# A three-layer transformer block on one core: attention heads of two layers taken in pairs on the two halves of TensorE's rows

## What is computed

```
s_loc = einsum('bnqkgd,bnjkd->bnkgqj', qb, kw) * scale        # windowed; masked outside |q - k| <= 128
s_ctx = einsum('bnqkgd,bckd->bnkgqc', qb, kc) * scale
p = softmax(concatenate([s_loc, s_ctx, sink]))
o = einsum('bnkgqj,bnjkd->bnqkgd', p_loc, vw) + einsum('bnkgqc,bckd->bnqkgd', p_ctx, vc)
...
x_new = x + g1 * (concatenate([ya, yb, yc, yd]) @ w_out)      # yc windowed, yd global
```

## Time and profile before

| | us |
|---|---|
| median of 3 runs (lowest to highest) | 2987.54 (2985.93 to 2989.95) |
| the profiled execution | 2986.1 |
| its span | 2984.3 |
| TensorE busy | 2711.7 (91%) |
| VectorE busy | 1300.7 (44%) |
| ScalarE busy | 970.9 (33%) |
| POOL busy | 333.7 (11%) |
| mean granted TensorE clock | 0.943 |

### The profile page before, as it was taken

The page is one execution under the profiler, slowest core; times in us unless marked ns, Lnnn a source line. Parts: engine busy times, 40 slices in busy tenths (PEclk is TensorE's granted clock), DMA queues, the critical chain, the costliest instruction groups (busy, mean ns, idle before and its releaser), DMA issues.

```text
span 2984.3 us, 35383 instructions
## 1 busy us (share of the span) xinstructions
PE 2711.7 (91%) x13904; PEld 1548.5 (52%) x13904; DVE 1300.7 (44%) x2556; ACT 970.9 (33%) x1825; POOL 333.7 (11%) x185
## 2 busy tenths in 40 slices
PE   5999999699999998697897999998699997899998
PEld 3875554322333332585544333332277686787886
DVE  2496532434444444385523332232566555343342
ACT  4224431234344433524512222221324334322222
POOL 0210002001111111120010000000013321122221
PEclk9998989799999999797998999999899998999999
DMA  6216631599999999320024999999421002222221
GB/s 239 71 43 219 233 114 52 194 317 350 343 353 359 359 352 332 103 85 1 1 99 180 386 386 387 387 386 386 171 86 57 8 15 78 69 94 99 85 92 50
DMA packets 303260, 568.51 MB, mean 191 GB/s; under 512 B 12656, under 2 KB 55792, under 8 KB 302968
## 3 DMA queue, kind: packets, MB, share of 16 engines
q1 hardware_dynamic: 294480, 545.33, 51.5%
q0 software_dynamic: 3840, 12.59, 1.8%
q10 hardware_dynamic: 4776, 8.33, 0.8%
HBM read 551.53 MB, written 14.68 MB: 190 GB/s over the span
## 4 chain that ended last, share of the span: by engine, by line
PE 71%; DVE 6%; DMA 5%; ACT 3%; issue 2%; POOL 0%; ACTq 0%; DVEq 0%; SPq 0%
PE PS L958 21%; PE PS L964 6%; PE PS L907 5%; PE PS L1061 4%; PE PS L1060 4%; PE PS L1059 4%; PE PS L1072 2%; PE PS L1012 2%; PE PS L1074 2%; PE PS L1073 2%; PE PS L1049 2%; PE PS L725 2%; DMA WIDE<-in_w_gate_dram 1%; PE PS L883 1%; PE PS L870 1%
## 5 line engine op out<-in xcount | busy, mean ns | idle before, releaser
L958 PE MATMUL PS<-RING,RF 128*64 128x512 f32 x1448 | 353.5, 614 | 12.1 <-DMA RING<-in_w_up_dram 4.0
L958 PE MATMUL PS<-WIDE,RF 128*64 128x512 f32 x1408 | 331.9, 601 | 8.8 <-DMA WIDE<-in_w_up_dram 3.2
L2526 POOL TENSOR_TENSOR WHL<-RING,WHL 128x1024 fp32r<-128x1024 f32 x57 | 153.8, 2697 | 1240.7 <-ACT WHL L1292 1240.7
L958 PEld LDWEIGHTS PS<-RING,RF 128*64 128x64 f32 x1448 | 93.0, 138 | 221.6 <-issue 202.3
L1059 PE MATMUL PS<-RR,WHL 128*128 128x512 f32 x512 | 203.9, 398 | 1.1 <-DVE RR L2279 1.1
L1061 PE MATMUL PS<-RR,WHL 128*128 128x512 f32 x512 | 204.3, 399 | 0.0
L1060 PE MATMUL PS<-RR,WHL 128*128 128x512 f32 x512 | 202.0, 395 | 0.0
L958 PEld LDWEIGHTS PS<-WIDE,RF 128*64 128x64 f32 x1408 | 92.7, 137 | 203.9 <-issue 185.0
L1292 ACT ACTIVATE WHL<-RING 128x1024 fp32r<-128x1024 f32 (+1 forms) x115 | 119.7, 1045 | 176.2 <-PE PS L1074 101.9
L1523 ACT ACTIVATE RF<-PS,MODS,MSC 128x128 f32<-128x128 f32 x192 | 77.2, 437 | 302.9 <-PE PS L1012 156.1
L1775 DVE TENSOR_TENSOR WHL<-RING,WHL 128x1024 fp32r<-128x1024 f32 (+1 forms) x58 | 71.6, 1234 | 196.2 <-ACT WHL L1292 196.2
(11 more groups left out here) (383 smaller groups left out, 4997.2 us busy)
## 6 DMA issues: line engine op xcount, KB each, us to landing
RING<-in_w_gate_dram SPq DMA_DIRECT2D x83, 1024.0 KB
WIDE<-in_w_down_dram SPq DMA_DIRECT2D x74, 1024.0 KB, 8.2
RING<-in_w_up_dram SPq DMA_DIRECT2D x70, 1024.0 KB
WIDE<-in_w_up_dram SPq DMA_DIRECT2D x57, 1024.0 KB, 12.4
RING<-in_w_down_dram SPq DMA_DIRECT2D x51, 1024.0 KB
RING<-in_ada_w_dram SPq DMA_DIRECT2D x48, 1024.0 KB
WIDE<-in_w_gate_dram SPq DMA_DIRECT2D x45, 1024.0 KB, 11.2
RING<-in_w_in_dram SPq DMA_DIRECT2D x30, 1024.0 KB
```

The lines of the kernel that those rows point to most:

```text
L958: ins = e.matmul(a[r:r + 64, :], xs[:, j, 0:64], w[:, i, :], start=j < 2, stop=j > 5)
L2526: e.tensor_tensor(lo, load_buffer(loads[st["load"]])[:, js, cs], h.bitcast(F32), ALU.subtract).then_inc(pool, G(("lo", st["i"])))
```

## The change

Heads are taken as pairs (0, 2) and (1, 3), which lie on rows 0 to 63 and 64 to 127, and both score matmuls of a pair are issued next to each other. The plan goes by pairs: one turn n of the loop appends the head entry of items 2n and 2n + 1, sums of the pair before, flip of its first item, both middles, ada 0 and 1, one background entry that may take a bank, flip of its second item, ada 2, values of the pair before that, a background entry that in layer 1 may not take one of the ring's banks, ada 3. Statistics get six buffers. The output's halves now hold heads (0, 2) and (1, 3), for which the host lays out the rows of `w_out` in that order.

```diff
-    items = [(m, t, h) for m in range(2) for t in range(T if need_ctx else 4) for h in range(4)]
+    items = [(m, t, h) for m in range(2) for t in range(T if need_ctx else 4) for h in (0, 2, 1, 3)]
...
-        while need_ctx and now[0] % 2 == 0:
+        while need_ctx and now[0]:
             yield
...
-    for i in range(len(items) + 3):
...
+    pairs = len(items) // 2
+    for n in range(pairs + 2):
+        i = 2 * n
+        now[0] = 0
+        if 0 < n <= len(units):
+            plan.append(("ada", *units[n - 1], 4))
...
+        if n < pairs:
+            plan.append(("head", i, *items[i]))
+        if 0 < n <= pairs:
+            plan += [("sum", i - 2, *items[i - 2]), ("sum", i - 1, *items[i - 1]), ("flip", i - 2, *items[i - 2])]
+        if n < pairs:
+            plan += [("middle", i, *items[i]), ("middle", i + 1, *items[i + 1])]
+        if n < len(units):
+            plan += [("ada", *units[n], 0), ("ada", *units[n], 1)]
+        next(later, None)
+        if 0 < n <= pairs:
+            plan.append(("flip", i - 1, *items[i - 1]))
+        if n < len(units):
+            plan.append(("ada", *units[n], 2))
+        if n > 1:
+            plan.append(("values", i - 3, *items[i - 3]))
+        now[0] = 1
         next(later, None)
         if n < len(units):
+            plan.append(("ada", *units[n], 3))
...
-        STATS = [SM[:, 64 + 4 * i:68 + 4 * i] for i in range(4)]
+        STATS = [SM[:, 64 + 4 * i:68 + 4 * i] for i in range(6)]
...
-                        sc = bank(scores, ("score", l, i), (A, ("exp", l, i)))
+                        sc = [bank(scores, ("score", l, i + r), (A, ("exp", l, i + r))) for r in range(2)]
...
+                        for own in (True, False):
+                            for r in range(2):
+                                rs = slice(64 * r, 64 * r + 64)
+                                q = QKT[m][rs, h, 128 * t:128 * t + 128]
+                                if not own:
+                                    e.matmul(sc[r][:, 512:768], q, QKT[m][rs, 2, 512:768], start=True, stop=True
+                                             ).then_inc(pe, P(("score", l, i + r)))
+                                elif wl:
+                                    e.matmul(sc[r][:, 512 - wl:512], q, QKT[m][rs, 2, 128 * b0:128 * b1], start=True, stop=True)
...
-                        v0 = 512 * m + 384 + 64 * (h // 2)
+                        v0 = 512 * m + 384
...
-                                ins = e.matmul(o[64 * r:64 * r + 64, 0:128], QKV[:, b, v0:v0 + 64],
+                                ins = e.matmul(o[64 * r:64 * r + 64, 0:128], QKV[:, b, v0 + 64 * r:v0 + 64 * r + 64],
...
-                        if i > 3:
-                            e.wait_ge(pe, P["pv", l, i - 4 + (i + 1) % 2])
+                        if i > 5:
+                            e.wait_ge(pe, P["pv", l, i - 6 + (i + 1) % 2])
...
-                        e.tensor_tensor(YT2[:, 2 * m + h // 2, 128 * t:128 * t + 128], o[:, 0:128], SHARE[i // 2 % 2],
+                        e.tensor_tensor(YT2[:, 2 * m + h % 2, 128 * t:128 * t + 128], o[:, 0:128], SHARE[i // 2 % 2],
```

More of the change, by code:

```diff
@@ L269, in attention_plan @@
     nd = next(i for i, it in enumerate(items) if it[0] == 1)
-    for i in range(len(items) + 3):
-        now[0], n = i, i // 2
-        if i % 2 == 0 and 0 < n <= len(units):
+    pairs = len(items) // 2
[3 more added lines that the diff above has]
+        if 0 < n <= len(units):
             plan.append(("ada", *units[n - 1], 4))
-        if i % 2 and n < len(units):
-            plan.append(("ada", *units[n], 2))
         if i == nd:
@@ L278, in attention_plan @@
                 next(later)
[L279 to L282, removed]
+        if n < pairs:
[14 more added lines that the diff above has]
+        now[0] = 1
         next(later, None)
         if n < len(units):
-            plan.extend([("ada", *units[n], 3)] if i % 2 else [("ada", *units[n], q) for q in range(2)])
+            plan.append(("ada", *units[n], 3))
+    now[0] = 0
+    for _ in later:
+        pass
+    return plan
     for _ in later:
@@ L850, in attend @@
                         i, m, t, h = k
-                        rs, g = slice(64 * (h // 2), 64 * (h // 2) + 64), h % 2
-                        q = QKT[m][rs, g, 128 * t:128 * t + 128]
                         b0, b1 = span(m, t)
                         wl = 128 * (b1 - b0)
-                        sc = bank(scores, ("score", l, i), (A, ("exp", l, i)))
+                        sc = [bank(scores, ("score", l, i + r), (A, ("exp", l, i + r))) for r in range(2)]
                         e.wait_ge(act, A["qkT", l, m, 5])
[L857 to L860, removed]
+                        for own in (True, False):
[7 more added lines that the diff above has]
+                                    e.matmul(sc[r][:, 512 - wl:512], q, QKT[m][rs, 2, 128 * b0:128 * b1], start=True, stop=True)
                     elif what == "flip":
@@ L888, in attend @@
                             ins = e.matmul(o[64 * r:64 * r + 64, 128:256],
-                                           STATS[(i - 1 + r) % 4][:, 2:3].to_broadcast([128, 64]), IDN, start=True, stop=True)
+                                           STATS[(i - 1 + r) % 6][:, 2:3].to_broadcast([128, 64]), IDN, start=True, stop=True)
                         ins.then_inc(pe, P(("pv", l, i)))
@@ L1410, in attend @@
                         wl = 128 * (b1 - b0)
-                        st, eb = STATS[i % 4], EB[i % 3]
+                        st, eb = STATS[i % 6], EB[i % 3]
                         e.wait_ge(dve, V["neg", l, i])
@@ L2021, in attend @@
                         wl = 128 * (b1 - b0)
-                        sc, st = held("score", l, i), STATS[i % 4]
+                        sc, st = held("score", l, i), STATS[i % 6]
                         e.wait_ge(pe, P["score", l, i])
@@ L2030, in attend @@
                         e.wait_ge(dve, V.n)
-                        if i > 3:
-                            e.wait_ge(act, A["exp", l, i - 4])
+                        if i > 5:
+                            e.wait_ge(act, A["exp", l, i - 6])
                         e.tensor_reduce(st[:, 0:1], sc[:, 512 - wl:768], AX.X, ALU.max).then_inc(dve, V())
@@ L2051, in attend @@
                         i, m, t, h = k
-                        st = STATS[i % 4]
+                        st = STATS[i % 6]
                         if m == 0:
@@ L2701 @@
         rows += [g["q_norm_g"][l]] * 4 + [g["k_norm_g"][l]] * 2
+    by_half = [np.arange(64) + 64 * h for h in (0, 2, 1, 3)]
+    by_half = np.concatenate([np.arange(512)] + [512 + 256 * m + hr for m in range(2) for hr in by_half])
     con, hc, bias = tables()
@@ L2707 @@
         "consts": con, "hconst": hc, "bias": bias,
-        "x": g["x"][0], "ctxt": g["ctx"][0], "ada_w": g["ada_w"], "w_in": g["w_in"], "w_out": g["w_out"],
+        "x": g["x"][0], "ctxt": g["ctx"][0], "ada_w": g["ada_w"], "w_in": g["w_in"], "w_out": g["w_out"][:, by_half, :],
         "router": np.pad(g["router_w"], ((0, 0), (0, 0), (0, 16))), "w_gate": g["w_gate"], "w_up": g["w_up"], "w_down": g["w_down"],
```

## The result

The changed kernel takes 2943.7 us (median of 4 runs, 2940.7 to 2948.4), the kernel before, run beside it, 2986.7 us (2980.7 to 2990.0): a ratio of 0.9863, 95% interval [0.9843, 0.9883]. That is faster by 1.4%, more than the 0.6% forecast (2970 us) and just under the low end of the range, 2944. The profiled execution took 2940.7 us with a span of 2938.9, 45.4 less than the span before.

The account below looks back on a forecast made before the run. Attention was taken as bound by loops of waits between engines, TensorE full only in places. Layer 1's 216 us plus layer 2's 129 gave 345 against 362.5, 17.5 less: 2968.6 profiled, 2970 us forecast, range 2944 to 2998.

Parts of the forecast that it names:

- The clock, layer 1: Layer 1's attention: 195.5 us at full clock becomes 216 with 30% at half clock, 4 us more than before.
- the clock holds: Rival, chance 0.23: layer 1 at half clock only a tenth of the time, both attention stages 37 us less, 2950 us.
- The sign that I had named for it: Sign that the forecast is wrong: layer 1's attention shorter than 200 us or longer than 230.
- What an us at half clock costs: Layer 1's attention: time at half clock does its work slower by a factor of 1.45.
- Heads at half: Score matmuls on two row halves run side by side in half the time: 45 us less of TensorE, 25 in layer 1.
- The halves don't overlap: Rival, chance 0.08: heads cost TensorE what they cost before; 16 us slower, 3003 us.
- Bank 6: Layer 1: values wait for the PSUM bank behind ScalarE's copy and exponentials; a spread step takes 9.4 us, TensorE idle 1.3.
- The slower rival: Rival, chance 0.15: bank 6 waits put layer 1 at half clock two thirds of the time; 20 us slower, 3007 us.
- Layer 1's other steps: Layer 1's attention at full clock: parts of 71.5, 68, 37 and 19 us, sum 195.5.
- Layer 2: Layer 2's attention: 129 us, 21 less than before.
- The keys part: Layer 2, heads 4 to 15: VectorE sets steps of 8.0 to 8.5 us; 47 us, 14 less than before.
- Costed at nothing: Statistics columns, copies, masks, table loads, output-weight layout and modulation transfers add no time; transfers at their limit in shortest steps.

Follow-up runs that it names:

- a2: The changed kernel again, unaltered, run for comparison: 2944.4 us, 0.9854 of the kernel before.
- e1: Changed kernel with both heads of a pair on the same half of the rows, one after the other (order alone): 2989.2 us, ratio 1.0013 to the kernel before.
- e12: Kernel before, with each score matmul contracting all 128 rows (other scores, another output): 2964.9 us, ratio 0.9935 to the kernel before.
- e11: Changed kernel with every score matmul issued twice, halves still side by side: 2976.0 us, ratio 0.9972 to the kernel before.
- e3: Kernel before, in its order by single items, with two heads issued on the two halves every second turn: 3126.8 us, ratio 1.0468.
- e5: Kernel before, with two unread 512-column products ahead of layer 2's windowed heads from the fourth on: 2981.1 us, ratio 0.9980.
- e10: e1 with each score matmul contracting all 128 rows (another output): 2968.8 us, ratio 0.9946 to the kernel before.
- e6: Changed kernel with layer 1's keys and spread entries, which take PSUM bank 6, ahead of the two middles: 2935.0 us, 0.9834 of the kernel before.
- e9: Changed kernel with a pair's four score matmuls issued one head after the other: 2939.7 us, ratio 0.9845 to the kernel before.
- e8: Pair plan and halves in layer 2 only; layer 1 as before, single heads on alternating halves: 2962.5 us, 0.9923 of the kernel before.

## Why the prediction was right or wrong

The sum was 27.9 us too high against the profiled execution (2968.6 forecast, 2940.7 taken). In its own terms:

- **The clock, layer 1: the step that failed, 14 us.** It said "I take the share of time at half clock as 30% where it was 25% over layer 1", because "the new steps have gaps" and 25 us less TensorE work. The gaps came (idle time 6% to 17%), the share at half clock fell to 10% (20 of 197 us). With 10% the same sum gives 202 instead of 216: that is the rival "the clock holds", 2950 us, which had a chance of 0.23 and describes what happened. My error was the step "the granted clock is low wherever TensorE has gaps", read off. The sign that I had named for it came true: layer 1 was shorter than 200 us (197.4, though 200.7 in a2). What the runs show in its place: with the same idle share the clock is 0.89 where heads contract 64 rows one after the other and 0.94 where they contract 128 (e1, e12), and it is 0.95 where two halves work at once (the changed kernel, e11). Long gaps do lower it too (e3, waits over 5 us, 0.74), and filling them with products on 128 rows lifts it (e5). The Trainium skill (TensorE: Matmul & The Clock Gate, Part 1) says that activity releases the throttle; by these runs a head on 64 rows, though it counts as busy in the profile, does less for that than one on 128 rows. That this is also why the changed kernel's clock rose is argued. Nearest to showing it is e11 against e1, with the same order and about the same time in the heads: 22 + 14 us at half clock side by side, 49 + 45 one after the other. e11 issues twice as many head products, though, and why the chip grants its clock by rows stays open.
- **What an us at half clock costs: right, as far as it was measured.** The sum took 1 − 1/1.45 = 0.31 us for each. e10 against e1: 47 fewer, 12.3 saved in the stages, 0.26 each; e12 against before: 58 fewer, 19.5 saved, 0.34 each. With 3 us between single traces, these two are the same.
- **Heads at half: right.** "Run side by side they take half": 65.8 to 33.0 us of busy time in layer 1. "Starting within a few ns of each other": the first records lie 6 ns apart. "The halves don't overlap" fell.
- **Bank 6: right, mechanism and size.** A spread step of "9.4 us" measured 9.5, with TensorE idle 0.9 behind L1384 where 1.3 was forecast. "The heads' 1.5 us are paid back to the bank": part three has four pairs, so 6 us less of heads, and is 35.4 us against 37.0; most was paid back. Taking the wait out gives 7 us (e6). The slower rival's place was right; its price wasn't, as the clock did not fall.
- **Layer 1's other steps: 4.6 us too long** (202 to 197.4 at the measured share). Parts three and four were at the full clock, and shorter than their sums for it: 35.4 for 37 and 17.8 for 19; the rest, 1.8, lies in the first two parts.
- **Layer 2: 4.3 us too long** (129 forecast, 124.7 measured). Its parts: 16.5 for 17, 42.2 for 47, 56.7 for 57, 9.3 for 8. The keys part is the whole error: a step is VectorE's work, as forecast, but 7.4 us, not 8.0 to 8.5. Two of its terms were too large: copies and product, 1.0 forecast, take 0.8 start to start, and the rotation's second half, 0.8 forecast, takes 0.55; the durations of the earlier trace rows overlap when nothing waits between them. The half us put on top of the 8.0 did not come either. The step with the scale took 12.8 for 13, the sigmoid's 8.6 for 9.3, a plain one 6.4 for 6.3. VectorE's wait for the values copy, "gone" by the forecast, fell only from 81.6 to 64.5 us over both layers: gone in the keys steps, still there elsewhere, where VectorE isn't what bounds.
- **Costed at nothing.** The rest of the program took 5.0 us less in this execution, mostly its own spread (above). The modulation's transfers did not become a bound: 228 to 241 GB/s at a share of 0.66 to 0.69. What I did not foresee is the fourth modulation stage's 9.5 us behind ScalarE's copy L1320, TensorE's largest wait in layer 1 besides bank 6.
- **The range** left out the result by 0.3 us. It should have reached to the clock rival with its own spread, which at a chance of 0.23 is the case next to the forecast.

## What to carry to other kernels

Split a change into its parts before you price it: here the order alone was worth nothing, the halves alone cost 4.7%, and both together gained 1.4%. The halves need an order in which a pair need not wait for the exponential of the item just before (over 5 us a pair in e3), and the order needs shorter heads to pay for the waits that it puts behind ScalarE's copies (in e1's layer 1, 7.9 us before the fourth modulation stage and 7.1 before the values; the kernel before had 0.0 and 0.6). When TensorE is "busy" at a low granted clock, look at how many of the 128 rows each product uses before you blame gaps; here two products of 64 rows side by side came with both the shorter heads and the higher clock. And where a shared PSUM bank is freed by a copy, put the copy ahead of the exponentials in the queue: here that was worth about another 0.3% (2935.0 us).

## What was not expected of the hardware

- A score product on 128 rows instead of 64, with the same columns and order, made the whole kernel some 20 us *faster* (e12, e10), with a higher TensorE clock (0.82 to 0.92 in layer 2's attention, e12).
- Products on the two halves of the rows pass each other: in e9 the second head's own product started 13 ns after the first head's, ahead of a context product issued before it, and the time did not change.
- Adding two products of 512 columns on 128 rows per head (e5) took 6.5 us off a stretch of 61.1.
- A low clock need not cost: layer 2's first part took 16.5 us at 0.58 in the changed kernel and 16.2 us in e8, whose half-clock time there was half as long. TensorE is idle 38% of that part in the changed kernel.
